# One single-core kernel, its SBUF map laid out in another order

## The reference

```
x = x + rms_norm(gla_mixer(rms_norm(x)));   x = x + rms_norm(sq_relu_mlp(rms_norm(x)))
x = x + rms_norm(swa_sink_mixer(rms_norm(x))); x = x + rms_norm(sq_relu_mlp(rms_norm(x)))
x = layer_norm(alpha*x + even_mixer(x));    x = layer_norm(alpha*x + swiglu(x))
x = layer_norm(alpha*x + odd_mixer(x));     x = layer_norm(alpha*x + swiglu(x))

def sq_relu_mlp(h, w_up, w_down):           # w_up 1024 x 4096, w_down 4096 x 1024
    return jnp.square(jax.nn.relu(h @ w_up)) @ w_down
def swiglu(x, w_gate, w_up, w_down):        # 1024 x 2816, twice, and 2816 x 1024
    return (jax.nn.silu(x @ w_gate) * (x @ w_up)) @ w_down
```

## Time and profile before

| | us |
|---|---|
| three runs | 2483.84, 2483.87, 2495.47 |
| median | 2483.87 |
| the profiled execution, its own time | 2483.87 |
| its span in the trace | 2481.7 |
| PE busy | 2430.3 |
| POOL busy | 1088.6 |
| ACT busy | 946.1 |
| DVE busy | 724.7 |

### The profile page before, as it was taken

The page is one execution under the profiler, slowest core; times in us unless marked ns, Lnnn a source line. Parts: engine busy times, 40 slices in busy tenths (PEclk is TensorE's granted clock), DMA queues, the critical chain, the costliest instruction groups (busy, mean ns, idle before and its releaser), DMA issues.

```text
span 2481.7 us, 29800 instructions
## 1 busy us (share of the span) xinstructions
PE 2430.3 (98%) x11691; PEld 1984.9 (80%) x11691; DVE 724.7 (29%) x1289; ACT 946.1 (38%) x1896; POOL 1088.6 (44%) x893
## 2 busy tenths in 40 slices
PE   8999999999999999999999999999999999999998
PEld 7867888887867888887885788888888767888887
DVE  2233420223374320214244441010152464210104
ACT  4523442433474432433444333323233553332231
POOL 4523544444403544454544444444454402544443
PEclk9999999999999999999998999999999999999999
DMA  5312333332202333332320233333233201433332
GB/s 174 85 51 64 91 97 98 98 98 81 77 27 80 96 97 98 98 97 90 106 81 26 81 103 97 98 98 97 86 101 86 69 1 60 124 98 98 98 97 74
DMA packets 161395, 215.62 MB, mean 87 GB/s; under 512 B 38199, under 2 KB 86095, under 8 KB 161255
## 3 DMA queue, kind: packets, MB, share of 16 engines
q1 hardware_dynamic: 157632, 203.65, 27.4%
q10 hardware_dynamic: 3623, 10.07, 1.3%
HBM read 211.00 MB, written 2.10 MB: 86 GB/s over the span
## 4 chain that ended last, share of the span: by engine, by line
PE 92%; DVE 4%; POOL 2%; ACT 1%; issue 1%; DMA 0%; ACTq 0%; DVEq 0%; POOLq 0%
PE PS L333 14%; PE PS L335 14%; PE PS L334 14%; PE PS L339 13%; PE PS L341 13%; PE PS L340 13%; PE PS L1364 3%; PE PS L1347 1%; PE PS L414 1%; PE PS L2138 1%; POOL WL L306 1%; PE PS L2130 1%; DVE X L654 1%; PE PS L993 1%; PE PS L1466 0%
## 5 line engine op out<-in xcount | busy, mean ns | idle before, releaser
L306 POOL TENSOR_TENSOR WL<-WS,WH 128x512 fp32r<-128x512 f32 (+2 forms) x788 | 1004.5, 1282 | 1221.0 <-ACT WH L299 1216.9
L299 ACT ACTIVATE WH<-WS 128x512 fp32r<-128x512 f32 (+2 forms) x788 | 479.6, 615 | 1237.8 <-PE PS L341 631.1
L333 PE MATMUL PS<-AH,WH 128*128 128x512 f32 (+1 forms) x1712 | 641.3, 375 | 4.1 <-DVE AL L449 2.9
L334 PE MATMUL PS<-AL,WH 128*128 128x512 f32 (+1 forms) x1712 | 638.3, 373 | 0.0
L335 PE MATMUL PS<-AH,WL 128*128 128x512 f32 (+1 forms) x1712 | 638.2, 373 | 0.0
L333 PEld LDWEIGHTS PS<-AH,WH 128*128 128x128 f32 x1712 | 325.6, 190 | 62.7 <-issue 6.6
L334 PEld LDWEIGHTS PS<-AL,WH 128*128 128x128 f32 x1712 | 325.5, 190 | 55.5 <-issue 0.5
L335 PEld LDWEIGHTS PS<-AH,WL 128*128 128x128 f32 x1712 | 325.3, 190 | 55.6
L341 PE MATMUL PS<-WH,h_HL 128*128 128x512 f32 x864 | 336.1, 389 | 0.0
L339 PE MATMUL PS<-WH,h_HH 128*128 128x512 f32 x864 | 336.1, 389 | 0.0
L340 PE MATMUL PS<-WL,h_HH 128*128 128x512 f32 x864 | 336.1, 389 | 0.0
(11 more groups left out here) (315 smaller groups left out, 2018.6 us busy)
## 6 DMA issues: line engine op xcount, KB each, us to landing
WS<-in_mlp_w_up_dram SPq DMA_DIRECT2D x128, 256.0 KB, 2.8
WS<-in_mlp_w_down_dram SPq DMA_DIRECT2D x128, 256.0 KB, 2.6
WS<-in_ffn_w_gate_dram SPq DMA_DIRECT2D x176, 128.0 KB, 2.1
WS<-in_ffn_w_up_dram SPq DMA_DIRECT2D x176, 128.0 KB, 2.2
WS<-in_ffn_w_down_dram SPq DMA_DIRECT2D x88, 256.0 KB, 2.6
WS<-in_gla_w_in_dram SPq DMA_DIRECT2D x48, 256.0 KB, 2.7
WS<-in_even_w_in_dram SPq DMA_DIRECT2D x48, 256.0 KB, 2.7
WS<-in_odd_w_in_dram SPq DMA_DIRECT2D x32, 256.0 KB, 2.7
```

The lines of the kernel that those rows point to most:

```text
L299: e.activation(WH[:, s, 0:n], WS[:, s, 0:n], ACT.Copy).then_inc(hi.sem, hi.tick(i))
L306: e.tensor_tensor(WL[:, s, 0:n], WS[:, s, 0:n], WH[:, s, 0:n].bitcast(F32), ALU.subtract).then_inc(lo.sem, lo.tick(i))
L333: e.matmul(o, h, xh[:, cs], start=start, stop=False, skip_group_check=free)
L334: e.matmul(o, h, xl[:, cs], start=False, stop=False, skip_group_check=free)
```

## The change

The diff reorders the SBUF map and nothing else. X, Y and TB go from the end of the map to its beginning. In the weight ring, WS now stands ahead of WH and WL. The shared area of the stages goes from the beginning to the end, where it takes all that is left (72736 bytes in place of 72704). The regions laid over it, and over GB, take the new limits. Offsets in bytes within a partition, as the two programs allocate them:

| tensor | length | before | after |
|---|---|---|---|
| X | 16384 | 188352 | 16512 |
| Y | 16384 | 204736 | 32896 |
| TB | 8192 | 221120 | 49280 |
| AH | 16384 | 89216 | 57472 |
| AL | 16384 | 105600 | 73856 |
| WS | 12288 | 146560 | 90240 |
| WH | 12288 | 121984 | 102528 |
| WL | 12288 | 134272 | 114816 |
| CK | 3648 | 158848 | 127104 |
| GB | 12288 | 176064 | 144320 |
| shared area (HH first) | | 16512 | 156608 |

```
-        s_off = base[0]
-        base[0] += ROOM
-        s_end = base[0]
+        X = sb("X", [P, NT, D])
+        y_off = base[0]
+        Y = sb("Y", [P, NT, D])
+        tb_off = base[0]
+        TB = sb("TB", [P, 2, D])
         ah_off = base[0]
         AH = sb("AH", [P, 8, T], F32R)
         al_off = base[0]
         AL = sb("AL", [P, 8, T], F32R)
+        WS = sb("WS", [P, NS, RW])
         WH = sb("WH", [P, NS, RW], F32R)
         WL = sb("WL", [P, NS, RW], F32R)
-        WS = sb("WS", [P, NS, RW])
...
         GB = sb("GB", [P, 3, D])
-        gb_end = base[0]
-        X = sb("X", [P, NT, D])
-        y_off = base[0]
-        Y = sb("Y", [P, NT, D])
-        tb_off = base[0]
-        TB = sb("TB", [P, 2, D])
-        assert base[0] <= end, base[0] - end
+        s_off = base[0]
+        room = end - s_off
+        assert room >= 16 * T * 8 + 4096, room
...
-        take = region("h_", s_off, s_end)
+        take = region("h_", s_off, end)
...
-        take = region("eg_", gb_off, gb_end)
+        take = region("eg_", gb_off, s_off)
```

More of the change, by code:

```diff
@@ L27 @@
 RW = 512
-ROOM = 72704
 C_ID, C_PW, C_TRIB, C_TRI, C_ONE, C_NEGM, C_SWA = 0, 128, 144, 272, 400, 528, 656
@@ L174, in program @@
         HT = take("HT", [P, 2, T])
-        take = region("g_", s_off, s_end)
+        take = region("g_", s_off, end)
         gQ = take("Q", [P, 4, T])
@@ L186, in program @@
         gBL = take("BL", [P, 2, 4, 8])
-        take = region("s_", s_off, s_end)
+        take = region("s_", s_off, end)
         sQ = take("Q", [P, 16, T], F32R)
@@ L193, in program @@
         sPT = take("PT", [P, 3, 512])
-        take = region("e_", s_off, s_end)
+        take = region("e_", s_off, end)
         eXS = take("XS", [P, NT, D])
@@ L215, in program @@
         eTM = at("e_TM", al_off + 3 * T * 4, [P, 2, T])
-        take = region("o_", s_off, s_end)
+        take = region("o_", s_off, end)
         oQ = take("Q", [65, 8, T])
@@ L227, in program @@
         oFR = at("o_FR", tb_off + (D + T) * 4, [8, T])
-        take = region("og_", gb_off, gb_end)
+        take = region("og_", gb_off, s_off)
         oS = take("S", [P, 4, 512])
```

## The result

The changed kernel takes 2503.76 us (median of 9 runs, 2500.41 to 2510.04); the kernel before, measured beside it, 2491.55 us (9 runs, 2482.97 to 2495.49). The ratio is 1.0059 with a 95% interval of 1.0044 to 1.0075, so 14.7 us slower, between 11.0 and 18.7 (the two medians alone differ by 12.2). I had forecast no change with 90% and a range up to 2496: the change is slower, and the time lies outside. All ratios here are of fast runs; one run of the kernel before took 4191 us at a mean granted clock of 0.58 and is not in them.

A forecast was written before the change was run, and what follows sets the result against it. PE's pace was taken to bound the kernel. The profiled execution's 2483.87 us plus terms of 0 for PE's reads, weight steps, DVE closes and transfers gave 2484 us, with a range from 2477 to 2496 us.

The forecast's parts named there:

- What bounds the kernel: Whole kernel: PE's pace sets the time, with 92% of the span on PE and 0.2267 us per 512-column matmul.
- The slack of the weight steps: Weight stream: ACT's copies and POOL's subtractions have 11.6 us of slack, so new addresses cost 0, within 0.4 us.
- the DVE closes: Sublayer closes, DVE and POOL on X, Y and TB: 0 us, with bounds of 16 us on either side.
- the transfers: DMA of weights, behind the slack, and of X at the start: 0 us, with 1.3 us either side for the start.
- PE's reads: Weight products, 6864 matmuls of 512 columns: operands at new addresses cost 0 us more.
- The bounds of that term: PE's reads: nothing below, +31.6 us above, from a first-mixer stretch at 0.2313 us a step against 0.2267.
- slower rival: Weight stream: PE's operand reads meet ACT, POOL and DMA accesses; steps up to 0.2313 us, 2515.5 us in all; 5%.
- faster rival: Sublayer closes: long DVE instructions are address conflicts and go, saving 16.0 us, 2467.9 us in all; 4%.

The follow-up runs named there:

- ring_off64: Only WS, WH and WL moved to 64 bytes past a multiple of 128, against the kernel before; ratio 1.0149 (1.0119 to 1.0180).
- the low and the high map: Low: kernel before, shared area moved up 64 or 128 bytes, ratios 1.0070, 1.0044. High: changed kernel as is, 1.0059, or its shared area moved up 64 bytes, 1.0042.

## Why the prediction was wrong

- **What bounds the kernel** was right: PE's pace is the time. 6.67 ns in 2591 steps and 0.6 us in 96 more are 17.9 us, where the ratio has 14.7 (11.0 to 18.7). The value of 2484 was also low for the kernel before itself: beside the change it measured 2491.55, so 7.7 of the 19.8 us between 2484 and 2503.76 are the spread of the kernel before, and do not come from the change.
- **The slack of the weight steps** was right, as were the values of 0 for ACT, POOL, the DVE closes and the transfers; the durations in their rows stand.
- **PE's reads, "so I take 0"** is the step that failed. I argued from two stretches and six slots that the address does not count: AH at 89216, WH at 121984, HH at 16512, slots 2048 and tiles 512 bytes apart. (The 146560 of the text is WS, which PE does not read.) All of these are 128 past a multiple of 256. The evidence varied the height of the operands and never the thing that decides, their place within 256 bytes against each other, and the change moved exactly that, from d = 0 to d = 64 for the shared area. The runs showed 233.34 ns a step in place of 226.67 there, 17.3 us on the term that I had put at 0. I had worked out this remainder for WS and its DMAs, and had not done so for HH. That 864 records have one duration was a statement on one value of d.
- **The bounds of that term**, 0 to 31.6 us, did hold the measured 17.3, by luck. Their upper end came from a stretch at d = 0: in finer times the 8 steps of the earlier trace rows, which follow a step of 337 ns, are 230, 231, 236, 228, 233, 231, 226 and 227 ns, a disturbance that passes within six steps. And 6864 leaves out the 1752 matmuls of 512 columns with AH, AL, e_PH or e_PL loaded. I then chose the lower end and let the range follow the choice, with two thirds of the slower rival's distance cut off.
- **The slower rival** had the right place (PE's operand reads in the weight stream) and the wrong partner. Nothing that ACT, POOL or a DMA does is needed: the cost is whole in the 2.1 us in which PE is alone, the pace of kind "F" is the same in the same map, beside the same copies, and a shift of one PE operand against the other brings and takes the cost. At 5% it was rated too low: that I had no row with another d was a reason for doubt and not for zero.
- **The faster rival** did not happen; the long DVE instructions are at their places, as the pair of 1.73 and 0.69 us shows.
- **The Trainium skill**, in "SBUF — State Buffer", section "Who interferes with whom", gives PE two read ports, one for the moving operand and one for LDWEIGHTS, independent of each other, and lets PE wait on nobody. I used the section against both rivals. That PE does not wait for other engines' reads and writes agrees with the runs: the step is 0.2333 us beside the copies and without them. Between PE's own two reads they disagree: the mean step is 226.67, 228.90, 232.39 or 233.3 ns by where the two operands stand to each other. The measurement decides.

What stays open is the mechanism inside. That the two reads meet in some structure of 256 bytes fits the table but for one row, and no run looks into it. The one is ring_off64 at d = 192, with 228.9 and 233.3 ns in one trace, where what ran just before a stretch seems to count. At d = 0 a disturbance passes, as in the earlier trace rows; in the kernel after, at d = 64, the steps of 231 and 236 ns go on to the end of every stretch on HH and HL.

## What to carry over

When tensors are laid out anew, compare for each matmul the starts of its loaded and its moving operand modulo 256 bytes, before and after; in a stream of back-to-back matmuls keep them equal. Here 192 bytes of padding give back all that the new map cost. Of the six offsets tried, 0 has the best pace for 512 columns; for 256 columns the one other offset seen, 64, was 3.8 ns a step faster, so the rule is one for 512 columns. And ask of rows that seem to prove an independence which values they covered: six slots and three tensors with one remainder are one sample.

## What the runs showed of the hardware

- With a float32r load of 128 x 128 and 512 moving columns, the mean step between matmuls is 226.67 ns at d = 0, 228.90 at 192 (233.3 in three stretches of ring_off64), 232.39 at 128 and 233.3 at 32, 64 and 224. At d = 0 it is the same wherever in the partition the loaded tensor lies (16512 or 156800) and with all operands 64 past a multiple of 128; for other d this was not varied by itself, but at d = 64 and 128 the low and the high map agree.
- The cost is there with PE as the only reader: 9 steps in 2.10 us at the end of the kernel after.
- With 256 columns the mean step is 119.9 ns at d = 0 and 116.1 at d = 64 (ring_off64).
- The cost is not additive over loads: 13.3 ns for each off load when one in three is off, 6.7 when all are.
- The recorded load is 188 ns in all of these; the cost shows in the step and in the matmul's duration (389, 396).
- The granted clock in the last attention is at its lower level for 0, 13.7, 17.1 or 20.5 us, and the stage takes 109.5, 115.5, 117.1 or 118.8 us. At d = 0 both 0 and 17.1 occur.
